# Two landing waits per eight gathers on GpSimd in a two-layer decoder with product-key experts

## The reference

```python
def one_chunk(xc):                      # 128 tokens
    q = (xc @ w_query).reshape(C, PEER_HEADS, 2, PEER_KEY_DIM)
    s = jnp.einsum('chpd,hpnd->chpn', q, subkeys)
    ...                                 # top 16 of 16 x 16 candidates: idx, top_s
    gate = jax.nn.softmax(top_s, axis=-1)
    act = jax.nn.gelu(jnp.einsum('chkd,cd->chk', u_tbl[idx], xc), approximate=False)
    coef = gate * act
    return jnp.einsum('chk,chkd->cd', coef, v_tbl[idx])
```

## Time and profile before

| | |
|---|---|
| time, median of 3 runs (lowest, highest) | 1553.29 us (1553.16, 1553.7) |
| the profiled execution: time, span | 1554.89 us, 1553.1 us |
| busy, share of the span: PE, DVE, ACT, POOL | 67%, 67%, 26%, 63% |
| moved by transfers, mean rate | 607.57 MB, 391 GB/s |
| chain that ended last: DMA, PE, POOL, DVE | 35%, 21%, 17%, 14% |
| mean granted clock of TensorE | 0.826 |

### The profile page before, as it was taken

How to read it: one execution, slowest core, us unless ns; L and a number is a source line. 1 busy time by engine, 2 the same in 40 slices (tenths; PEclk the granted TensorE clock), 3 DMA queues, 4 the chain that set the end, 5 groups by cost and what they waited for, 6 DMA issues and landing times.

```text
span 1553.1 us, 13591 instructions
## 1 busy us (share of the span) xinstructions
PE 1035.4 (67%) x4216; PEld 471.9 (30%) x4216; DVE 1036.3 (67%) x2716; ACT 397.5 (26%) x920; POOL 974.2 (63%) x1041
## 2 busy tenths in 40 slices
PE   9998877655846767736675688787757774444444
PEld 8984422221213332212221334333212221111111
DVE  3367667775777484837676757377778677767673
ACT  1122132222222323222321232333222332112122
POOL 0067757776766655756666665467757767777772
PEclk9999978887967987878887788988979787766667
DMA  9699999999999999999999999999999999999996
GB/s 330 200 343 391 406 406 409 407 406 403 409 409 406 398 405 402 382 407 405 407 406 404 385 401 402 396 373 409 406 406 409 409 410 409 410 409 409 409 409 243
DMA packets 194636, 607.57 MB, mean 391 GB/s; under 512 B 17596, under 2 KB 44292, under 8 KB 194564
## 3 DMA queue, kind: packets, MB, share of 16 engines
q0 software_dynamic: 147456, 536.94, 87.3%
q1 hardware_dynamic: 46976, 69.73, 12.7%
q10 hardware_dynamic: 132, 0.04, 0.0%
HBM read 605.59 MB, written 1.05 MB: 391 GB/s over the span
## 4 chain that ended last, share of the span: by engine, by line
DMA 35%; PE 21%; POOL 17%; DVE 14%; issue 8%; ACT 5%; DVEq 0%; POOLq 0%; ACTq 0%
DMA rows<-in_peer_u,expert 18%; DMA rows<-in_peer_v,expert_v 16%; POOL rows L682 10%; PE sums L967 8%; DVE rows L1820 7%; POOL rows L675 7%; PE banks L783 4%; PE banks L799 4%; DVE coef L1837 2%; ACT soft_diag L1346 1%; PE banks L792 1%; PE sums L792 1%; DMA wring<-in_attn_w_q 1%; PE banks L775 0%; ACT L1331 0%
## 5 line engine op out<-in xcount | busy, mean ns | idle before, releaser
L967 PE MATMUL sums<-rows,soft_diag 128*64 128x512 f32 x2048 | 583.6, 724 | 446.9 <-ACT soft_diag L1346 446.6
L1820 DVE SCALAR_TENSOR_TENSOR rows<-rows,xn_near 128x1024 f32<-128x1024 f32 x512 | 612.6, 1219 | 253.3 <-DMA rows<-in_peer_u,expert 241.3
L682 POOL DMA_INDIRECT rows<-in_peer_v,expert_v x512 | 489.6, 956 | 295.4 <-PE sums L967 159.0
L675 POOL DMA_INDIRECT rows<-in_peer_u,expert x512 | 481.9, 941 | 258.9 <-issue 126.5
L967 PEld LDWEIGHTS sums<-rows,soft_diag 128*64 128x64 f32 x2048 | 162.7, 164 | 841.9 <-ACT soft_diag L1346 541.1
L1346 ACT ACTIVATE soft_diag<-stacked,coef 128x64 f32<-128x64 f32 x512 | 160.7, 343 | 369.8 <-DMA rows<-in_peer_v,expert_v 296.7
L1338 ACT ACTIVATE gelu<-dots 128x8 f32<-128x8 f32 x64 | 13.3, 208 | 446.1 <-DVE rows L1820 444.2
L799 PE MATMUL banks<-wring,xT 128*128 128x512 f32 x160 | 77.3, 636 | 3.4 <-DMA wring<-in_attn_w_q 3.4
L1837 DVE SCALAR_TENSOR_TENSOR coef<-gelu,gate_inv,gate 64x4 f32<-64x4 f32 x256 | 56.8, 222 | 23.4 <-ACT gelu L1338 19.5
L1885 DVE SCALAR_TENSOR_TENSOR soft_diag<-banks,soft_diag 128x512 f32<-128x512 f32 (+1 forms) x8 | 7.7, 958 | 92.7 <-ACT soft_diag L1367 92.7
L783 PE MATMUL banks<-xT,rows 128*128 128x128 f32 x448 | 51.1, 276 | 1.3 <-issue 0.6
(11 more groups left out here) (230 smaller groups left out, 958.6 us busy)
## 6 DMA issues: line engine op xcount, KB each, us to landing
wring<-in_w_kv SPq DMA_DIRECT2D x14, 1024.0 KB, 16.9
rows<-in_peer_u,expert POOLq DMA_INDIRECT x512, 15.0
rows<-in_peer_v,expert_v POOLq DMA_INDIRECT x512, 14.4
wkept<-in_peer_w_query SPq DMA_DIRECT2D x8, 1024.0 KB, 13.7
rows<-in_conv_w_in SPq DMA_DIRECT2D x7, 1024.0 KB, 11.9
wring<-in_peer_w_query SPq DMA_DIRECT2D x7, 1024.0 KB, 13.1
wring<-in_attn_w_q SPq DMA_DIRECT2D x7, 1024.0 KB, 16.5
wkept<-in_conv_w_out SPq DMA_DIRECT2D x4, 1024.0 KB, 12.5
```

What stands on the lines that cost most here:

```text
L675: nc.gpsimd.indirect_dma_start(u_row[j], None, u_table, bass.IndirectOffsetOnAxis(ap=expert[n % 2][:, k:k + 1], axis=0)).then_inc(u_landed ...
L682: nc.gpsimd.indirect_dma_start(v_row[j], None, v_table, bass.IndirectOffsetOnAxis(ap=expert_v[n % 2][:, k:k + 1], axis=0)).then_inc(v_land ...
L967: last = nc.tensor.matmul(sums[side * HP:(side + 1) * HP, half, :], diag[:, g * GROUP + j, :], v_row[j][:, half * 512:(half + 1) * 512], s ...
L1820: nc.vector.scalar_tensor_tensor(out=u_row[j], in0=u_row[j], scalar=1.0, in1=xn_near[:, :, :].rearrange("p a d -> p (a d)"), op0=ALU.mult, ...
```

## The change

In every group after the first, GpSimd waits twice in the eight u gathers and twice in the eight v gathers until an earlier gather has landed: before place 0 for place 3 of the half before, and before place 4 for place 7 of the half before. The halves follow one another as u, v, u, v. No wait is taken away, and no gather changes its place.

```diff
--- before.py
+++ after.py
@@ -55,6 +55,7 @@
     NH = CH * HEADS
     STEPS = LAYERS * NH
     GROUPS = TOPK // GROUP
+    IN_FLIGHT = GROUP // 2
     assert (CH, KEYS, KD, COLS) == (2, P, P, 2 * P) and GROUPS == 2 and D == PAIRS * P and KT == PAIRS
     W_EARLY = (U_SLOTS + V_SLOTS) // 2
     assert U_SLOTS == GROUP and V_SLOTS == GROUP and TAPS == 3 and LAYERS == 2
@@ -708,11 +709,19 @@
                 elif g == 0:
                     pool.wait_ge(expert_ready, n + 2)
                 for j in range(GROUP):
+                    if j == 0:
+                        pool.wait_ge(v_landed[IN_FLIGHT - 1], 16 * K)
+                    elif j == GROUP // 2:
+                        pool.wait_ge(v_landed[GROUP - 1], 16 * K)
                     pool.wait_ge(dot_done, GROUP * (K - 1) + j + 1)
                     gather_u(n, g, j)
                 if g == 0:
                     pool.wait_ge(expert_v_ready, n + 1)
                 for j in range(GROUP):
+                    if j == 0:
+                        pool.wait_ge(u_landed[IN_FLIGHT - 1], 16 * (K + 1))
+                    elif j == GROUP // 2:
+                        pool.wait_ge(u_landed[GROUP - 1], 16 * (K + 1))
                     if j % 2 == 0:
                         pool.wait_ge(v_used, TWOS * (K - 1) + j // 2 + 1)
                     gather_v(n, g, j)
```

## The result

The changed kernel takes **1575.62 us** in the median (1569.82 to 1575.82, 5 runs) against 1553.7 us for the kernel before (5 runs): the ratio is 1.0131, interval 1.012 to 1.0143. It is 21.9 us slower. The forecast was 1555.0 with a range up to 1566.0, so the time lies outside the range, on the side of rival A.

What follows compares the result with a forecast made beforehand. The prediction took transferred bytes to bound the kernel: profiled 1554.89 us, plus 0 steady state, 1.3 first throttled gather and 0.4 instructions, gave 1556.6; 1.6 lower for the median of runs, 1555.0 us. Range 1552.0 to 1566.0.

Steps and rivals of the forecast that it cites:

- rival A: First gathers of four, 120 to 1500 us: under load a gather needs over 6.13 us, so slower; chance 0.27.
- What bounds the kernel, and that the waits bind: Whole run: bytes set the end, at 409 GB/s late; nine to eleven gathers are queued, so new waits nearly always bind.
- The cost of a wait in the steady state: All fours after the start: landings still follow 1.28 us apart, so the added waits cost nothing.
- the wake-up: On GpSimd, from a wait's release to the gather's start: 0.27 us, leaving 6.13 us from issue to landing.
- Instructions: The 252 added waits are separate semaphore instructions, 16 KB more to fetch: between nothing and 0.9 us, taken as +0.4.
- the need: Time a gather needs from issue to landing: at least 5.1 us; with 5.5 to 5.6 us landings keep the full rate.
- The margin of 0.5 to 0.6 us: Steady state: the 6.13 us left from issue to landing exceeds the 5.5 to 5.6 us needed.
- The first throttled gather: Next u gather after group 0 starts at 105.4 us instead of 103.39, leaving a hole: +1.3 us (1.1 to 1.5).
- The existing waits: GpSimd's slot waits, 159.0 us for TensorE and 51.8 for VectorE, shrink as new waits replace them: no loss or gain.
- Both of its signs: Late stretch below 405 GB/s, and VectorE's products in fours with a longer step between them.
- 387 GB/s in the shallow stretch: Rate over 91 to 112 us, before GpSimd got ahead, against 409 later; put mostly down to GpSimd's slower issues.
- Rival B: Shared K and V weight blocks, 16.9 us each, get through sooner with fewer gathers queued: 1546.5 us; chance 0.08.

Runs made afterwards that it cites:

- four back: Changed kernel with each landing wait asking for the landing four gathers back instead of five: 1723.69 us against 1554.18, ratio 1.1091.
- the waits behind the others: Changed kernel with all 252 landing waits placed after the other waits of their gather: 1595.22 us against 1553.93, ratio 1.0266.
- Six gathers back: Changed kernel with all landing waits after their gather's other waits, asking six gathers back instead of five: 1554.85 us against 1554.41.

## Why the prediction was wrong

**What bounds the kernel, and that the waits bind:** right. The depth fell from eleven to under five gathers (6.2 / 1.28).

**"The cost of a wait in the steady state", taken at nothing:** this is the step that failed, in two of its numbers. The first is the wake-up. 0.27 us came from a single row, a wait that its gather carried, and was put on all 252. At 62 of them it is 0.75 us, because the wait for the indices comes first in the program and takes the gather's own place. So there a gather has 6.4 - 0.75 = 5.65 us and not 6.13. That the added waits stand in semaphore instructions of their own was written down in the prediction, under "Instructions", and priced as fetched bytes; what it does to the way from a release to the gather was not asked.

The second is the need. The two gathers of the earlier trace rows with 5.5 and 5.6 us were read as an upper bound, since each landed at its time. They show only that the late gather itself lands in time. The changed kernel loses at the one after: 1352.30, 1353.77, 1355.70. The bound would have had to be read two gathers further on, and the trace of before already had the sign. Behind the gather of 100.91 us, the one of 102.15 us took 6.0 us and landed at 108.1, 1.75 us after it and not 1.28:

```profile
102.15 0.93 POOL L682 DMA_INDIRECT rows<-in_peer_v,expert_v  x1 [0.30 <-issue]
```

Nor were the 5.1 us of the run's first gather a least time. In the changed kernel the gathers of 105.85 and 1391.40 us landed 4.2 us after their issue, and the ones behind them came late all the same. The time from issue to landing is therefore no fixed need: a late gather lands sooner, and the loss appears in those that follow.

The margin of 0.5 to 0.6 us was thus none at the 62 places: their late gathers cost 13.9 us, 0.22 us each on average, where the prediction had put nothing. And even with the short wake-up everywhere, and the 6.15 us that it leaves, 4.6 us are lost. That part of "nothing" failed too, and its cause is open.

**"The first throttled gather", +1.3 us:** right in kind and place, small in size. GpSimd's timeline there in the changed kernel:

```profile
101.91 0.94 POOL L683 DMA_INDIRECT rows<-in_peer_v,expert_v  x1 [0.30 <-issue]
105.85 0.97 POOL L676 DMA_INDIRECT rows<-in_peer_u,expert  x1 [3.00 <-issue]
107.12 0.94 POOL L676 DMA_INDIRECT rows<-in_peer_u,expert  x1 [0.31 <-issue]
```

The gather starts at 105.85 us and not at 105.4, again because three waits come together. It landed at 110.1 us, earlier than the 110.5 to 110.9 of the prediction; the next one landed 2.7 us after it and the one behind that another 1.7 us later. The hole costs 2.3 us (0.6 to 3.4 by the interval) when measured alone. As at the other places it is the gathers behind the late one that are late.

**"Instructions", +0.4 us:** nothing measurable (0.9998, 0.9989 to 1.0007), which does not exclude 0.4 us.

**"The existing waits", neither loss nor gain:** right. They shrank and the landing waits took their place.

**Rival A** named the mechanism: the need is above what the issue leaves. Both of its signs came, 395 GB/s in the late stretch and longer steps between the products. Its price was x for each of 126 pairs of fours, with x the same everywhere. Most of it came at a quarter of the places, and there the four gathers took 5.6 us in the median instead of 5.1. It had a chance of 0.27, but half of it was put below 12 us, and the range ended there; 387 GB/s in the shallow stretch was the better witness and should have weighed more. By the latency of HBM at high load in the Trainium skill, "DMA: Bandwidth & Descriptors", section "Latency and other measured facts", the prediction's estimate of the time was 1652 us: the need of 6.9 us is too much, since with 6.15 us the loss was only 4.6 us (3.3 to 7.0). The same page's fit in section "Anatomy of one DMA — SWDGE (gpsimd) path", by which an estimate for a gather is 3.2 us, is too little: by it four back would have cost nothing, and they cost 169.5 us. The same page's rule in section "Rules for kernel authors", to issue early and wait late, holds in this case, from five gathers down.

**Rival B** is out: the blocks of the shared K and V weights took 15.9 us instead of 16.9, and nothing came of it.

## What to carry to other kernels

A wait that limits how many transfers are under way is free only as long as the depth covers the way from landing to landing: wake-up, issue and transfer. In this kernel that is six gathers of 1.28 us; with five it depends on tenths of a microsecond, and with four each wait costs 0.67 us. Before such a wait is added, its release should be traced through the instruction that carries it. Where several waits come together ahead of one gather, as here, the one that is released last should be the first in the program, so that the instruction carries it itself. And a row that shows a late transfer landing in time is not a bound until the ones behind it have been read too.

## What the runs showed of the hardware

- GpSimd starts a gather 0.26 us after the release of a wait that the gather carries, and 0.75 to 0.79 us after that of a wait in a semaphore instruction ahead of it. The order of the waits in the program decides which is which. With five gathers under way this difference was worth about 14 us of 1554, some 2.5 of them together with a pause at one gather.
- The first gather of the run, 128 rows of 4 KB, lands 5.1 us after its issue, and later ones that were issued late landed after 4.2 us. To keep landings 1.28 us apart the issue had to lie 5.6 us or more ahead (an estimate from the run with four back); below that the gathers behind it often come late.
- The cost is steep in depth: 169.5 us with four back, 21.9 with five, none that can be measured with six.
- GpSimd's pauses of 1.9 us without a wait come at fixed places: at gather 897 in six of the kernels, and with the waits behind the others also at 113, 309, 505 and 701. Six gathers back hide them.
